# A two-block transformer on one core: waits of TensorE taken apart, splits and loads moved, fillers in three more waits

## The reference

```
# block 1
h = rmsnorm(x, norm1_w);  p = h @ w_in            # q, k, v | qkv_g | z | a, b | gates
ya = diff_attention(...) @ w_proj_attn            # 8 heads, softmax 1 - lambda softmax 2
og = rmsnorm(scan_fwd + scan_bwd) * silu(z)       # gated delta rule, both directions
yg = og @ w_proj_gdn
x = x + (sigmoid(gate_a) * ya + sigmoid(gate_g) * yg) @ w_out
h2 = rmsnorm(x, norm2_w)
aff = softmax(h2 @ w_router)                      # 16 experts
top_val, top_idx = top_k(aff.T, 64)               # each expert takes 64 tokens
x = x + scatter(top_val * ((silu(xs @ w_gate) * (xs @ w_up)) @ w_down))   # 1024 -> 2048 -> 1024
x = rmsnorm(x, norm_f_w)
# block 2
h = rms_norm(x, pre_mix_g)
y_a = chunk_band_attention(...);  y_b = rwkv7_time_mix(...)   # 8 heads of 64 each
x = x + rms_norm((gate_a * (y_a @ proj_a) + gate_b * (y_b @ proj_b)) @ w_out, post_mix_g)
u = square(relu(rms_norm(x, pre_ffn_g) @ w_up)) @ w_down      # 1024 -> 4096 -> 1024
x = x + rms_norm(u, post_ffn_g)
```

## Time and profile before

| | us |
|---|---|
| runs shown | 3044.27, 3044.82, 3045.36 |
| median | 3044.82 |
| profiled execution | 3046.83 |
| its span | 3045.0 |
| TensorE busy | 2653.5 (87%) |
| VectorE busy | 915.8 (30%) |
| ScalarE busy | 759.6 (25%) |
| GpSimd busy | 582.7 (19%) |

### The profile page before, as it was taken

How to read it: one execution, slowest core, us unless ns; L and a number is a source line. 1 busy time by engine, 2 the same in 40 slices (tenths; PEclk the granted TensorE clock), 3 DMA queues, 4 the chain that set the end, 5 groups by cost and what they waited for, 6 DMA issues and landing times.

```text
span 3045.0 us, 33976 instructions
## 1 busy us (share of the span) xinstructions
PE 2653.5 (87%) x14319; PEld 1725.9 (57%) x14319; DVE 915.8 (30%) x1606; ACT 759.6 (25%) x1290; POOL 582.7 (19%) x173
## 2 busy tenths in 40 slices
PE   7989878878899798888898898888978889799998
PEld 5756767667456633323333333356757756678886
DVE  2357745653101301010110110123564521231221
ACT  3247642632111110100100100043341121332222
POOL 3310452542122100000000000021201122334342
PEclk9999979979899899999999999998978999899999
DMA  4300212203223489999999999943200032322322
GB/s 140 111 29 15 97 57 84 83 2 111 69 83 111 187 368 428 428 429 428 429 428 429 429 428 428 427 146 111 63 1 1 8 117 90 117 76 97 94 94 75
DMA packets 130851, 559.35 MB, mean 184 GB/s; under 512 B 7256, under 2 KB 88480, under 8 KB 103080
## 3 DMA queue, kind: packets, MB, share of 16 engines
q1 hardware_dynamic: 129864, 551.28, 45.7%
q0 software_dynamic: 864, 6.29, 0.5%
HBM read 547.01 MB, written 10.54 MB: 183 GB/s over the span
## 4 chain that ended last, share of the span: by engine, by line
PE 69%; DMA 13%; DVE 10%; ACT 5%; issue 3%; POOL 1%; DVEq 0%; SPq 0%; ACTq 0%; POOLq 0%
DMA S<-in_w_up 11%; PE PS L563 8%; PE PS L565 8%; PE PS L564 8%; PE PS L2043 7%; PE PS L2020 6%; PE PS L555 4%; PE PS L2005 2%; PE PS L3007 2%; PE PS L3133 2%; PE PS L3135 2%; PE PS L3136 2%; PE PS L2054 1%; PE PS L548 1%; DMA S<-in_w_down 1%
## 5 line engine op out<-in xcount | busy, mean ns | idle before, releaser
L2290 POOL TENSOR_TENSOR r_block<-S,r_block 128x2048 fp32r<-128x2048 f32 x57 | 262.0, 4596 | 1519.6 <-ACT r_block L2279 1510.9
L2020 PE MATMUL PS<-S 128*64 128x512 f32 x2048 | 458.4, 596 | 83.4 <-DMA S<-in_w_up 74.4
L563 PE MATMUL PS<-r_block,r_block 128*128 128x512 f32 x1040 | 418.4, 402 | 10.8 <-DVE r_block L536 4.7
L565 PE MATMUL PS<-r_block,r_block 128*128 128x512 f32 x1040 | 406.0, 390 | 0.0
L564 PE MATMUL PS<-r_block,r_block 128*128 128x512 f32 x1040 | 405.5, 390 | 0.0
L2020 PEld LDWEIGHTS PS<-S 128*64 128x64 f32 x2048 | 140.0, 137 | 394.1 <-issue 244.1
L489 POOL TENSOR_TENSOR r_block<-S,r_block 128x2048 fp32r<-128x2048 f32 x40 | 182.9, 4574 | 497.7 <-ACT r_block L481 488.8
L2043 PE MATMUL PS<-S 128*64 128x512 f32 x1024 | 223.9, 594 | 6.0 <-DMA S<-in_w_down 2.7
L563 PEld LDWEIGHTS PS<-r_block,r_block 128*128 128x128 f32 x1040 | 195.7, 188 | 57.9 <-issue 8.0
L564 PEld LDWEIGHTS PS<-r_block,r_block 128*128 128x128 f32 x1040 | 195.7, 188 | 45.2 <-issue 6.0
L565 PEld LDWEIGHTS PS<-r_block,r_block 128*128 128x128 f32 x1040 | 195.6, 188 | 41.5
(11 more groups left out here) (456 smaller groups left out, 3688.5 us busy)
## 6 DMA issues: line engine op xcount, KB each, us to landing
S<-in_w_gate SPq DMA_DIRECT2D x64, 2048.0 KB, 18.1
S<-in_w_up SPq DMA_DIRECT2D x64, 2048.0 KB, 21.3
S<-in_w_down SPq DMA_DIRECT2D x64, 2048.0 KB, 25.6
S<-in_w_in SPq DMA_DIRECT2D x57, 1024.0 KB, 5.2
S<-in_w_up SPq DMA_DIRECT2D x16, 1024.0 KB, 5.5
S<-in_w_down SPq DMA_DIRECT2D x16, 1024.0 KB, 4.7
S<-decay_rows SPq DMA_DIRECT2D x8, 1024.0 KB, 6.7
S<-in_w_out SPq DMA_DIRECT2D x8, 1024.0 KB, 5.1
```

Source lines behind the costliest of these rows:

```text
L563: pe.matmul(out, wh, r32(HT[:, dc, :]), start=(dc == 0), stop=False)
L565: mm = pe.matmul(out, wl, r32(HT[:, dc, :]), start=False, stop=(dc == DC - 1))
L2020: mm = pe.matmul(PS[c * CAP:(c + 1) * CAP, 2 + 2 * m + g, :], XE[:, 2 * q + r, e * CAP:(e + 1) * CAP], w[:, r, 1024 * g + 512 * c:1024 * g ...
L2290: pool.tensor_tensor(r32(w), w, rounded(WH[k % 2]), ALU.subtract).then_inc(sem("w2_low"), 1)
```

## The change

Waits are taken apart, so that TensorE waits for less at a time; splits are moved on ScalarE and GpSimd; three of the first chunks of experts get places of their own (`moe_once`), outside the ring; the first gather runs between the first gate chunks; fillers are added and halved. The comparison is with the numbers 1 to 64 and not 0 to 63, so that one subtraction can go.

```diff
-            if first: split_act(act, first)
+            if first: first()
-        def split_tile(pe, out, w, off, low):
+        def split_tile(pe, out, w, off, low, arrive=None):
             for dc in range(DC):
+                if arrive:
+                    pe.wait_ge(*count(arrive, dc + 1))
...
-            pe.wait_ge(*count("n1_lo", DC))
-                split_tile(pe, PS[:, p % 2, :], parts_of(("qk", p // 2)), P * (p % 2), HTL)\
+                split_tile(pe, PS[:, p % 2, :], parts_of(("qk", p // 2)), P * (p % 2), HTL, "n1_lo" if p == 0 else None)\
...
         def group_act(act, gr):
-                    if j % 2 == 0 and gi:
+                    if j % 2 == 0 and gi not in (0, 12):
         def group_pool(pool, gr):
-                split_pool(pool, ("g", gr, 0))
                 split_pool(pool, ("g", gr, 1))
         def head_norms_act(act, gr):
-            if gr:
-                split_act(act, ("z", 1))
+            split_act(act, ("z", 1) if gr else ("g", 1, 1))
+        def first_split_pool(pool, gr):
+            for d in range(2):
+                pool.wait_ge(*count(f"sc_r{d}", 3 * (gr + 1)))
+            split_pool(pool, ("z", 0) if gr else ("g", 1, 0))
         def GDN_POOL(pool):
                 if gr:
+                    first_split_pool(pool, 0)
                     low_parts_back(pool, 0)
         def gate_pool(pool):
+            first_split_pool(pool, 1)
             low_parts_back(pool, 1)
-            for j in range(4):
+            for j in range(1, 4):
                 split_pool(pool, ("z", j))
         def gate_act(act):
-                if h % 2 == 0 and h:
-                    split_act(act, after(("z", h // 2)) or ("m", 0, 2))
+                if h in (2, 4):
+                    split_act(act, ("z", h // 2 + 1))
...
+            split_act(act, ("m", 0, 2))
         def merge_pe(pe):
                     if k == 0 and m == 0:
                         pe.wait_ge(*count("ot_back", 16))
+                        pe.wait_ge(*count("z_silu", GH - 2))
+                    if k == 0 and m == 1:
                         pe.wait_ge(*count("z_og", GH))
                         pe.wait_ge(*count("z_silu", GH))
-            pe.wait_ge(*count("mg_lo", DC))
-            pe.wait_ge(*count("mg_done", 16))
+            pe.wait_ge(*count("mg_lo", DC // 2))
                 await_split(pe, ("o", j))
+                if j == 1:
+                    pe.wait_ge(*count("mg_lo", DC))
                 for tc in range(TC):
+                    if j == 0:
+                        pe.wait_ge(*count("mg_done", 13 + tc))
...
-        moe_ring = [M_MOE + s * MSLOT for s in (5, 2, 1, 4, 0, 3)]
-        FREE = ((("z_og", GH), ("z_silu", GH)), (("mg_proj", 26),), (("out_proj", 16),),
-                (("out_proj", 16),), (("out_proj", 12),), (("out_proj", 16),))
+        moe_ring = [M_MOE + s * MSLOT for s in (5, 2, 0, 1, 4, 3)]
+        moe_once = [E0, M_DYN + 25600, M_HT]
+        ONCE = {2: 0, 7: 1, 8: 2}
+        RING0 = (0, 1, 3, 4, 5, 6)
+        FIRST = MSLOTS + len(ONCE)
+        FREE = ((("z_og", GH), ("z_silu", GH)), (("mg_proj", 26),), (("mg_proj", 32),), (("out_proj", 12),),
+                (("out_proj", 16),), (("out_proj", 16),), (("out_proj", 16),), (("out_proj", 16),), (("ro_logits", 1),))
         def moe_loads(eng):
-                if k < MSLOTS:
+                if k < FIRST:
                     for name, value in FREE[k]:
                         eng.wait_ge(*count(name, value))
+                elif k < FIRST + MSLOTS:
+                    eng.wait_ge(*count("mo_used", RING0[k - FIRST] + 1))
                 else:
                     eng.wait_ge(*count("mo_used", k - MSLOTS + 1))
+            eng.dma_start(NORMF, a["rows"][0].unsqueeze(0).to_broadcast([P, D])).then_inc(sem("router_in"), 16)
...
-            sp.dma_start(NORMF, a["rows"][0].unsqueeze(0).to_broadcast([P, D])).then_inc(sem("router_in"), 16)
...
         def router_pe(pe):
+            keep_busy(pe, 5, 26)
             pe.wait_ge(*count("ro_slot", 1))
         def router_dve(dve):
-            dve.tensor_scalar(CUM[0:NE, :], CUM[0:NE, :], -1.0, None, ALU.add).then_inc(sem("ro_slot"), 1)
...
+            def first_gate():
+                pe.wait_ge(*count("mo_sel", 3))
+                for q in range(5):
+                    if q < 4:
+                        gather_block(gathered_first(2 * q), 2 * q)
+                        gather_block(gathered_first(2 * q + 1), 2 * q + 1).then_inc(sem("mo_gathered"), 1)
+                    if q:
+                        pe.wait_ge(*count("mo_x", 2 * q))
+                        gate_up(0, 0, 0, q - 1)
+            keep_busy(pe, 5, 4)
             pe.wait_ge(*count("ro_pos", 1))
-            gather(0)
+            first_gate()
...
-                    if name == ("u", 1):
-                        pool.wait_ge(*count("pn1_x", TC))
+                    if name == ("u", 0):
+                        pool.wait_ge(*count("n4_dg", TC))
...
-                keep_busy(pe, 6, 1)
+                keep_busy(pe, 6, 1, 128)
         def rout_pe(pe):
+            first_merge_pe(pe)
...
-                    mm = pe.transpose(PS[:, m % 2, block_of(tc)], YTOK[:, tc, block_of(m)], ident)
+                    mm = pe.transpose(PS[:, 2 + m % 2, block_of(tc)], YTOK[:, tc, block_of(m)], ident)
...
-            pe.wait_ge(*count("m2_lo", DC))
-            pe.wait_ge(*count("m2_done", 16))
+            pe.wait_ge(*count("m2_lo", DC // 2))
...
         def ffn_pe(pe):
+            pe.wait_ge(*count("o2_copied", 4))
+            keep_busy(pe, 0, 20)
         def ffn_act(act):
-            split2_act(act, ("u", 0))
-            norm_act(act, "n4", [("pn1_x", TC)], "pre_ffn")
+            norm_act(act, "n4", [("pn1_x", TC)], "pre_ffn", lambda: split2_act(act, ("u", 0)))
         def block2_pe(pe):
             pe.wait_ge(*count("x2_done", TC))
+            keep_busy(pe, 7, 10)
```

More of the change, by code:

```diff
@@ L518, in norm_act @@
             if first:
-                split_act(act, first)
+                first()
             norm_out_act(act, tag, weight)
@@ L550, in norm_pe, with keep_busy @@
                 mm.then_inc(sem(tag + "_tp"), 1)
+        def keep_busy(pe, bank, n, width=256):
+            for _ in range(n):
+                pe.matmul(PS[:, bank, 0:width], ident, const("mask4")[:, 0:width], start=True, stop=True)
         def feature_tile(pe, out, w, off, src):
@@ L1998, in is_last, with gathered, gathered_first, gather_block @@
             return isinstance(i, int) and i == PAIRS - 1
+        def gathered(dc):
+            return PS[:, dc // 4, (dc % 4) * P:(dc % 4 + 1) * P]
+        def gathered_first(dc):
+            return PS[:, (0, 1, 6, 7)[dc // 2], (dc % 2) * P:(dc % 2 + 1) * P]
         def experts_pe(pe):
+            def gather_block(out, dc):
+                for tc in range(TC):
+                    mm = pe.matmul(out, paired(tc, dc), SELR[:, tc, :], start=(tc == 0), stop=(tc == TC - 1))
+                return mm
             def gather(i):
@@ L2075, in body, with gates @@
                 turn_down(i, 1)
+            def gates(i, e):
+                pe.wait_ge(*count("mo_h", i * 4 + 2 * e))
+                for m in range(2):
+                    if not (is_first(i) and e == 0 and m == 0):
+                        for q in range(4):
+                            gate_up(i, e, m, q)
+            keep_busy(pe, 5, 4)
             pe.wait_ge(*count("ro_pos", 1))
-            gather(0)
+            first_gate()
             over_pairs(pe, body)
@@ L2729, in units_pe @@
                         .then_inc(sem("u_scores"), 1)
-        def keep_busy(pe, bank, n):
-            for _ in range(n):
-                pe.matmul(PS[:, bank, 0:256], ident, const("mask4")[:, 0:256], start=True, stop=True)
         def inverse2_pe(pe, hf):
@@ L3004, in merge2_pe @@
                         if m < 2:
-                            w, src = slot2(("m", k, m)), (YAT, YBT)[m]
-                            for dc in range(4):
-                                mm = pe.matmul(out, w[:, dc, P * j:P * j + P], src[:, dc, :],
-                                               start=(dc == 0), stop=(dc == 3))
+                            mm = half_tile(pe, k, m, j)
                         else:
@@ L3016, in merge2_pe @@
                 await_split2(pe, ("o", j))
+                if j == 1:
+                    pe.wait_ge(*count("m2_lo", DC))
                 for tc in range(TC):
+                    if j == 0:
+                        pe.wait_ge(*count("m2_done", 13 + tc))
                     out2_tile(pe, PS[:, 4 * half + tc, :], parts2(("o", j)), kh, tc).then_inc(sem("o2_proj"), 1)
```

183 lines of the change are left out of this document (106 added, 77 removed), and 12 rows, old and new, of the table CHAINS.

## The result

The changed kernel took 2965.3 us (2962.0 to 2965.8, four runs) against 3044.55 of the kernel before (four runs): a ratio of 0.9739 (0.9722 to 0.9756), 79 us faster. The profiled execution has a span of 2963.4 us in a time of 2965.6, so against the profiled execution of before (3046.83) 81.3 us were saved, where the sum said 89.7. A second set of runs of the same kernel gave 2962.65 us, 0.9736 (0.9723 to 0.975), with a profiled span of 2959.1.

The account below looks back on a forecast made before the run. TensorE, busy 87% of the span, was taken as the bound, except in the expert stage, bound by DMA. Eleven terms sum to 89.7 us: 3046.8 to 2957.1, less 2.0 against the median, 2955 us; range 2935 to 2985.

Parts of the forecast that it names:

- the likeliest case: The sum as worked out, 2955 us, with its own range 2945 to 2968 and a chance of 54%.
- merge: Merge start of block 1: the 13.9 us wait for `z_og` and a dip of 2.6 go, 16.5 us.
- both out projections: Start of each: four low parts awaited instead of eight, and the half clock behind goes; 7.3 and 7.4 us.
- n4: Norm n4: ("u",0) subtraction moved off the `pn1_x` scalings, 4.3 us; low parts 1.6; no clock gain from 20 fillers: 5.9.
- n3: Norm n3: ten fillers bring 64 passes from 9.62 to 7.4 us; with low parts, less a late split, 3.3.
- n1: One of three norms whose low parts are awaited one by one; 1.6 us at each.
- The expert stage: DMA-bound stream: three more ready chunks and an earlier first use give about 14 us, bounds 5 and 23.
- the tenth use: Expert stage: chunk 15 needs TensorE's tenth use; data then from 1104.6 us, 177 chunks at 4.92 us each.
- they cost nothing and have the gather at full clock: Router: 26 fillers take about 13 us in a wait of 16.0 and leave the gather at full clock.
- Rival (a): Fillers misfire at low clock: the router's 26 take 22.4 us, 7.5 late, n3's cost 4.2; 2969 us, 12%.
- ("m",0,0) of block 2: Sixteen of 32 passes move into TensorE's idle time ahead of the turns, the others at 27.47/64 us each: 9.8 us.
- The scans: GpSimd subtracts before the reloads: the 6.4 us waits go, low parts late next in the first; 11.3 and 8.0 us.

Follow-up runs that it names:

- the two experiments: Changed kernel with six chunks and not nine ready: 2970.8 us, 0.9763; changed kernel with all four gathered pairs ahead of the first gate chunk: 2963.2 us, 0.9728.

## Why the prediction was right, and where it was off

*What bounds the kernel, and the sum.* 2955 was forecast, 2965.3 measured, within 2935 to 2985 and, with the second set's 2962.65, inside the likeliest case's own 2945 to 2968. Six of the eleven terms came within 1 us in both executions: merge, both out projections, recurrent steps, n4, and n3. Of the 10 us between the forecast and the first median, some 6.3 lie in the terms, 1.8 in stretches that nothing edits, and 1.7 in the 2.0 taken off for the median, which lay only 0.3 below the profiled execution. The misses mostly point one way, so luck did little; it helped at n1, where 3.2 and 2.1 us came for 1.6: the norm's 64 passes took 8.90 and 9.96 us where they took 10.30 before, with nothing of them edited (8.90 to 10.36 over all profiles). Those worked out as "the wait, and the half clock behind it" held best: putting the waits together again cost 18 to 20.5 us, where the terms (7.3, 7.4 and three times 1.6) said 19.5.

*The expert stage, 14 forecast, 11 measured.* The sum ran through "the tenth use", which the two experiments bear out: 7.5 us for the three chunks, and nothing for the earlier first use. Three of its links were 1 us short each. The selection was counted at 1058.8 us, 18.3 behind the first turn; it took 19.56, since the four fillers behind the second turn ran at half clock (3.28 us) and held up the gather (18.5 in the profiles where they took 1.99): the step "they cost nothing and have the gather at full clock" failed. From there to the tenth use, 1057.65 + 2 x 3.48 = 1064.6, it took 45.7 us and not 44.7, the interleaved gather's 1 us. And from the tenth use to the last chunk 874.3 and not 873.2. Together they are 3.3 us (the working gave 14.5, rounded to 14). The last chunk came 52.3 us earlier, where I had said 59; the rest of that lies ahead of the router, mainly in the logits and heads below.

*The fillers.* Rival (a) was right in kind and too dear: it priced all 26 at half clock. The granted clock was 0.50 only up to 1002.7 us, for their first 2.5 us, and they took 12.66 us, near the prediction's 13. They ended 2.66 us early, and what counted was the idle time behind them; the misfire was that of the four. The other profiles bear this out. In five with 26 fillers these ended 1.8 to 2.3 us ahead of the turn, and the four behind it took 1.99 us (2.49 in the one at 2.27); in the other five they ended 2.7 to 3.0 us ahead of it, and the four took 3.28 to 3.66.

*("m",0,0) of block 2, 9.8 forecast, 7.4 and 8.1 measured.* The step that failed is that the 16 passes behind the turns would run at 27.47/64 each, 6.9 us; they took 8.70 and 8.83 behind a wait of 3.1, and 7.13 when this wait was covered.

*The scans, 11.3 and 8.0.* The mechanism held, the low parts were late next. Their 2.1 us of wait brought 1.7 of half clock in one execution, which I hadn't counted, and behind the second scan TensorE's own restart of 0.94 us stayed: 7.0 and 6.9 for 8.0.

*n4.* The price of the row was right (4.25 us), and so was the count of no clock gain: the 20 fillers were worth nothing, 29 were worth 1.6 to 2.4. By the rule of the Trainium skill, TensorE: Matmul & The Clock Gate, HAM oscillation, idle time sends the clock back to its lower level; at n4 the trace agrees (4.03 us idle, 9.01 and 9.76 us against 7.38). The split of ("u",0) costs VectorE 4.27 us (9.14 against 4.87), where GpSimd's instruction alone takes 4.52. That fits the lock of which the Trainium skill, SBUF — State Buffer, Who interferes with whom, speaks: the scaling that met GpSimd's instruction ended 1.1 us behind it.

*What the sum left out.* It took all that the change doesn't edit as fixed. It isn't: the logits' 32 matmuls took 5.94 and 6.03 us where they took 4.34 before, 1.6 lost, and the heads between third tile and the end of the second scan took 181.4 and 181.8 us where they took 179.1.

## What to carry to other kernels

A wait on the path costs its length and often a stretch of half clock behind it. Both can be priced from rows, the second as a range, since behind the shorter waits here (2.1 us) it came in some executions and not in others. Then ask what is late next at each freed start. A filler that ends well ahead of the operand can be worth nothing: 4.0 us ahead it was at n4, and 2.7 us ahead, at the router's turn, what stood behind ran at half clock. Count it against the trace once it has run, and mend its number. Where buffers run ahead of a stream, follow the use that restarts it for good, not the first (here the tenth, with nine chunks ready): a first use that comes earlier, like that of the interleaved gather, buys nothing.

## What the runs showed that I had not expected

The clock doesn't fall at the same places in each execution. In the 13 profiles that have the changed kernel's router, the stretch from the last out projection to the first turn takes either 8.1 to 8.5 us (seven) or 10.4 to 10.8 (six), and nothing between; the 32 matmuls of the logits make the difference (3.6 to 4.0 us or 5.9 to 6.3), and the four fillers behind the second turn are slow in those of the six that have them. The wait of 2.1 us for the low parts is followed by passes at half clock in some profiles and not in others, of the very same program. So a term of 1 to 2 us can't be read from one profile. The two spans of the changed kernel lie 4.3 us apart (2963.4 and 2959.1), so two kernels' spans can differ by that much without an edit: the gain of an edit is better read from its own stretch.

Narrower fillers soon stop paying: at 64 columns the steps, 6.47 us for 6.58, were bound by the data, and the matmuls behind them ran at half clock.
